# Gathering expert values by token and weighing them in 32-column matmul groups

## Chip, cores, metric

The kernel runs on one core of a Trainium2 chip. The metric is the device time of one execution, in microseconds (us), the median of the runs. Engines are called PE (matmuls), DVE (vector), ACT (scalar), POOL (GpSimd, which here issues the indirect DMAs) and SP (plain DMAs).

## What is computed

One step of a decoder layer for 1024 prompt tokens and 32 sample tokens. The change lies in the expert part alone:

```python
def peer(u, w_pq, sub_keys, exp_u, exp_v):        # 1056 tokens in blocks of 128
    q = (xb @ w_pq).reshape(128, 8, 2, 128)       # 8 heads, two half keys
    s = einsum('thpd,pnd->thpn', q, sub_keys)     # scores against 2 x 128 sub keys
    sv, si = lax.top_k(s, 16)
    comb = sv[:, :, 0, :, None] + sv[:, :, 1, None, :]
    cidx = si[:, :, 0, :, None] * 128 + si[:, :, 1, None, :]
    tv, ti = lax.top_k(comb, 16)
    eidx = take_along_axis(cidx, ti)              # 16 experts per token and head
    g = softmax(tv)
    ue, ve = exp_u[eidx], exp_v[eidx]             # rows of 1024 floats, of 16384 experts
    a = gelu(einsum('td,thkd->thk', xb, ue))
    return einsum('thk,thkd->td', g * a, ve)
```

Each token needs 128 rows of `exp_u` and 128 rows of `exp_v` (8 heads of 16 slots), 4 KB a row.

## The kernel before

The program is a row of stages, each closed by a barrier: loading, attention, convolution, merge, then `experts` (line 1486), then a last normalisation and output. `experts` works through tiles of 128 tokens, eight for the prompt. Token t of a tile sits in partition t. The 32 sample tokens are laid out four times over the partitions, each copy with two of the eight heads, so that the last tile needs only two heads' worth of rounds. That makes 66 units (a unit is one head of one tile), each with 16 gathers of `exp_u` and 16 of `exp_v`: 2112 gathers of 128 rows, 524288 bytes each.

For unit q the work is this. `score` (PE, line 1579) multiplies the tile by the head's folded key weights: 8 fp32 matmuls of 256 columns, each two instructions in the trace. `take_scores` (ACT, 1648) copies the bank. `pick` (DVE, 1714 to 1754) finds the best 16 of each half, forms 70 candidates, takes the best 16 and turns them into expert numbers. `gates` (ACT, 1654) takes the exponentials. Picks run a whole tile ahead of the gathers, since `advance_indices` (1766) hands over all eight heads at once.

`head` (POOL) first copies the unit's indices (1538), then issues 16 gathers into the ring `U` and then 16 into the ring `V` (both at line 1545). Both rings have 8 buffers. A gather for slot k brings one row for each of 128 tokens. It may start when the buffer of eight slots ago is free (`u_free`, `v_free`). POOL executes in order.

`dot` (DVE, 1798) multiplies each U buffer by the tokens and sums along the row, one instruction per slot, and releases the buffer. `weights` (ACT) takes the GELU (1659), DVE multiplies by the gates (1802), and ACT then makes a diagonal matrix per slot (1665, ring of 4). `weigh` (PE, 1589) multiplies that 128x128 diagonal by the V buffer: 2 fp32 matmuls of 512 columns per slot, which are four instructions in the trace, and releases the V buffer. The sum for the tile stays in two PSUM banks; `end` closes it (1600), ACT copies it (1671), PE turns it (1605), DVE adds it to `hT` (1808).

On DVE the order is pick of the unit eight ahead, then `dot` of this unit. On PE it is score, then `weigh`. All of this runs in hardware loops (`Fori`), most of it over heads within a tile. Another stage, `sample_attention`, already multiplies with a 32-column stationary operand into four partition quarters of one PSUM bank (line 999).

## Time and profile before

| What | Value |
|---|---|
| median of 3 runs | 5637.24 us (5636.52 to 5650.34) |
| profiled execution, first to last instruction | 5638.5 us |
| first and last gather of the expert stage start | 2003.97 us, 5379.93 us |
| PE, DVE, POOL busy over the span | 68%, 48%, 47% |
| DMA share, 3000 to 5300 us | 0.92, 329 GB/s |

The profile is of one execution. A timeline row gives start, duration, engine, line, operation, output and inputs and the count; the bracket is the idle time of the engine before it and what ended it. "issue" means that nothing the profile shows was waited for. Busy time of POOL for a gather is the time in which it writes the transfer's descriptors, not the transfer.

### The profile page before, as it was taken

Reading aid. Unit: us, or ns where it says so; the run is one execution under the profiler, and the core shown is the slowest. Engines: PE = TensorE matmul, PEld = TensorE weight load, DVE = VectorE, ACT = ScalarE, POOL = GpSimd, SP = SyncE. Lnnn points to the kernel's source line nnn. Section 1 sums busy time; section 2 is a strip of 40 time slices with the busy share of each in tenths; the row PEclk is TensorE's granted clock in tenths of the full one; section 3 lists DMA queues with packets and bytes.
Section 4 is the critical chain, followed back from the end, with each engine's and each line's share of the span. In section 5 each row is a group of like instructions: output and inputs, shape, how many; then the busy total and the mean of one; then the engine's idle time right before and its main releaser. Section 6 shows DMA issues by size and latency. Waiting matters only on the chain. (4 is left out here: it accounts for less than half of the span.)

```text
span 5638.5 us, 57052 instructions
## 1 busy us (share of the span) xinstructions
PE 3830.5 (68%) x14101; PEld 2341.2 (42%) x14101; DVE 2710.5 (48%) x8425; ACT 1038.5 (18%) x2091; POOL 2646.9 (47%) x2596
## 2 busy tenths in 40 slices
PE   6799854554997656676666666766666666766667
PEld 6667831322887523333333333333333333333246
DVE  2233275343112566555655565555555555555433
ACT  2122121111001211122121121121112111121121
POOL 2100222222112056666666666666666666666621
PEclk8855977777998777887888888888888878888879
DMA  2200166663112379999999999999999999999921
GB/s 62 73 23 12 37 227 221 225 237 106 57 46 61 98 253 331 333 327 323 333 331 325 331 328 332 328 327 335 333 324 328 325 329 329 330 328 333 329 90 50
DMA packets 471328, 1331.83 MB, mean 236 GB/s; under 512 B 48641, under 2 KB 141259, under 8 KB 471257
## 3 DMA queue, kind: packets, MB, share of 16 engines
q0 software_dynamic: 326240, 1180.32, 58.3%
q1 hardware_dynamic: 145024, 150.76, 8.7%
q8 instruction: 28, 0.46, 0.0%
q14 instruction: 36, 0.29, 0.0%
HBM read 1307.67 MB, written 23.66 MB: 236 GB/s over the span
## 5 line engine op out<-in xcount | busy, mean ns | idle before, releaser
L1589 PE MATMUL exp_ps_y<-exp_V,exp_diag 128*128 128x512 f32 x4224 | 1978.3, 632 | 1144.0 <-ACT exp_diag L1665 1125.5
L1798 DVE CUSTOM_DVE_ANT_0 exp_U<-exp_U,exp_x 128x1024 f32<-128x1024 f32 x1056 | 1294.4, 1226 | 1179.8 <-DMA exp_U<-in_exp_u,exp_idx_now 1154.9
L1589 PEld LDWEIGHTS exp_ps_y<-exp_V,exp_diag 128*128 128x128 f32 x4224 | 854.2, 204 | 2241.2 <-issue 1925.2
L1545 POOL DMA_INDIRECT exp_V<-in_exp_v,exp_idx_now x1056 | 1055.4, 999 | 735.5 <-PE exp_ps_y L1589 514.0
L1545 POOL DMA_INDIRECT exp_U<-in_exp_u,exp_idx_now x1056 | 1190.4, 1127 | 383.0 <-issue 312.2
L1665 ACT ACTIVATE exp_diag<-all_ident,exp_wt 128x128 f32<-128x128 f32 x1024 | 389.9, 398 | 1186.4 <-PE exp_ps_y L1589 1137.1
L1579 PE MATMUL exp_ps_sc<-ffn_wk,exp_ust 128*128 (+1 forms) x1152 | 276.4, 395 | 36.1 <-ACT exp_scores L1648 36.1
L1659 ACT ACTIVATE exp_act_dots<-exp_dots 128x16 f32<-128x16 f32 x66 | 14.2, 216 | 1384.4 <-DVE exp_dots L1798 1384.4
L1579 PEld LDWEIGHTS exp_ps_sc<-ffn_wk,exp_ust 128*128 128x128 f32 x1152 | 228.0, 199 | 96.6 <-issue 58.0
L1750 DVE SCALAR_TENSOR_TENSOR exp_picked<-exp_iota,exp_tif,exp_cidx 128x70 f32<-128x70 f32 x1152 | 252.8, 290 | 2.6
L999 PE MATMUL satt_ps_o<-satt_pages,satt_kT 128*32 128x512 f32 x512 | 92.8, 889 | 199.7 <-DMA satt_pages<-in_cache_v 197.5
L898 POOL DMA_DIRECT2D satt_pages<-in_cache_v x128 | 69.0, 539 | 249.6 <-issue 244.3
L958 PE MATMUL satt_ps_t<-all_ident,satt_pages 128*128 128x128 f32 x1024 | 130.0, 284 | 75.5 <-DMA satt_pages<-in_cache_k 37.8
L958 PEld LDWEIGHTS satt_ps_t<-all_ident,satt_pages 128*128 128x128 f32 x1024 | 117.0, 147 | 117.1 <-issue 53.6
L854 DVE SCALAR_TENSOR_TENSOR heads_yT<-convin_gp,all_wdw,heads_yT 128x1024 f32<-128x1024 f32 x120 | 153.3, 1278 | 0.0
L414 PE MATMUL merge_ps_b<-merge_x_high,merge_w_high 128*128 128x352 f32 x384 | 128.5, 335 | 28.8 <-POOL merge_w_low L366 28.8
L898 POOL DMA_DIRECT2D satt_pages<-in_cache_k x128 | 69.8, 546 | 165.6 <-issue 160.5
L655 PE MATMUL patt_ps_s<-patt_kh,patt_qh 66*128 66x512 f32 (+2 forms) x192 | 131.5, 823 | 20.8 <-DMA patt_kh<-k_rows 20.8
L364 POOL CAST merge_w_high<-merge_w 128x1024 fp32r<-128x1024 f32 x16 | 20.6, 1285 | 265.8 <-DMA merge_w<-in_w_in 265.8
L1137 POOL MEMSET convin_gp<- 128x120 f32 x1 | 0.2, 203 | 303.5 <-POOLq L116 303.5
L999 PEld LDWEIGHTS satt_ps_o<-satt_pages,satt_kT 128*32 128x32 f32 x512 | 23.9, 161 | 258.6 <-issue 258.6
L415 PE MATMUL merge_ps_b<-merge_x_low,merge_w_high 128*128 128x352 f32 x384 | 123.6, 322 | 0.0
(309 smaller groups left out, 5107.0 us busy)
## 6 DMA issues: line engine op xcount, KB each, us to landing
satt_pages<-in_cache_k SPq DMA_DIRECT2D x128, 256.0 KB, 4.1
satt_pages<-in_cache_k POOLq DMA_DIRECT2D x128, 256.0 KB, 4.3
satt_pages<-in_cache_v SPq DMA_DIRECT2D x128, 256.0 KB, 6.3
satt_pages<-in_cache_v POOLq DMA_DIRECT2D x128, 256.0 KB, 6.4
exp_U<-in_exp_u,exp_idx_now POOLq DMA_INDIRECT x1056, 6.1
exp_V<-in_exp_v,exp_idx_now POOLq DMA_INDIRECT x1056, 5.6
merge_w<-in_w_in SPq DMA_DIRECT2D x16, 512.0 KB, 4.0
keys_w<-in_w_pq SPq DMA_DIRECT2D x16, 512.0 KB, 4.9
```

Of the source, the lines that this page charges most:

```text
L414: pe.matmul(self.bank(j, c), w_high, x_high, start=first, stop=False)
L415: pe.matmul(self.bank(j, c), w_high, x_low, start=False, stop=False)
L655: last = pe.matmul(sbank[n % 2][:, c0:c1], qh[:, b, qb * P:(qb + 1) * P], kh[:, b, c0:c1], start=True, stop=True)
L854: ins = dve.scalar_tensor_tensor(out=y, in0=x, scalar=wc, in1=y, op0=ALU.mult, op1=ALU.add)
L898: eng.dma_start(ring[:, b, p, :], cache[0, ds(page, 1)].rearrange("a k h d -> k (a h d)"))\
L958: last = pe.transpose(tb[c][:, p * P:(p + 1) * P], ring[:, b, p, c * P:(c + 1) * P], sh.ident[:, :])
L1545: pool.indirect_dma_start(buf[:, k % size, :], None, table[0], bass.IndirectOffsetOnAxis(idx_now[:, hh, k:k + 1], 0))\
L1579: last = pe.matmul(scb[:, 0:2 * P].rearrange("p (a n) -> p a n", n=P), ust[:, k, :], wk[:, k, ds(2 * h, 2), :], start=k == 0, stop=k == KD ...
L1589: last = pe.matmul(yb[f][:, :], diag[:, k % ND, :], V[:, k % NV, f * 512:(f + 1) * 512], start=False, stop=False, skip_group_check=True)
L1665: act.activation(diag[:, k % ND, :], ident[:, :], ACT.Copy, scale=wt[:, k:k + 1]).then_inc(e["diag_ready"], 1)
L1750: st.did(dve.scalar_tensor_tensor(out=picked[:, k, :], in0=iota[:, :], scalar=tif[:, k:k + 1], in1=cidx[:, :], op0=ALU.is_equal, op1=ALU.mult,
L1798: dve.tensor_tensor_reduce(out=row, in0=row, in1=xb[:, :], scale=1.0, scalar=0.0, op0=ALU.mult, op1=ALU.add, accum_out=dots[:, k:k + 1]).t ...
```

## The change

Key gathers and dots stay as they are. Value gathers change from "slot k for 128 tokens" to "all 128 slots of one token", so that there are 1056 of them, as many as before. Expert numbers of a tile are transposed on PE (`turn_indices`) and copied to `idxT`, whose column is one token's list. The weights of a tile are transposed in the same way (`turn_weights`), and one ACT instruction per tile (`spread_weights`) writes them into `spread`, 4 groups of 32 matrices of 128x32 with one column that isn't zero. `weigh` now takes four tokens at once: 2 halves by 4 groups, each a matmul of 128x32 by 128x512 into its quarter of the bank. The diagonals, their 1056 ACT instructions and the copies of scores and indices fall away.

Everything is unrolled and ordered by ticks n of 16 slots. In tick n POOL alternates one key gather of unit n and one value gather, which is 136 gathers behind (`LAG`). PE does the score of unit n + 2, then four groups of `weigh`. ACT copies that score, then takes the GELU of unit n - 1 and the exponentials of unit n + 2. DVE does the pick of unit n + 2, the weights of unit n - 1, then the dots of unit n. The sample tile keeps two units; the four groups of its scores are now 32-row matmuls.

```diff
-    NU, NV, ND = 8, 8, 4
-    U0, V0, G0 = NU, NV + TOPK, 1
+    NU, NV = 8, 8
+    LEAD = 2
+    LAG = P + 8
     NC_ = 70
-
     blocks = [(0, 2, 16), (2, 8, 5), (8, 16, 1)]
+    NUNIT = PH * NT + 2
+    NROW = TOPK * NUNIT
+    NTOK = P * NT + NS
+    NTICK = (NTOK + LAG + TOPK - 1) // TOPK
+
+    def tile_of(n):
+        return min(n // PH, NT)
+
+    def last_unit(t):
+        return min(PH * t + PH, NUNIT) - 1
+
+    def tokens_to(t):
+        return min(P * t + P, NTOK)
...
+        spread = s.sb("spread", [P, 4, NS * NS])
         ysb = s.sb("y", [P, D])
-        scb = s.ps("sc")
+        scb, tb = s.ps("sc"), s.ps("t")
         xt = [s.ps(f"x{i}") for i in range(2)]
-        yb = [s.ps(f"y{i}") for i in range(2)]
...
+        yb = [[s.ps(f"y{b}{f}") for f in range(2)] for b in range(2)]
...
+        def v_begin(t):
+            return (P * t + LAG) // TOPK
+
+        def v_tick_of_end(t):
+            return (tokens_to(t) - 1 + LAG) // TOPK
+
+        def y_tick(t):
+            return v_tick_of_end(t) + 1
...
-            def head(n, col, hh):
-                hold(pool, e["v_free"], V0 + TOPK * (n - 1), e["passed_p"])
-                pool.tensor_copy(idx_now[:, hh, :], idx_cur[:, col]).then_inc(e["staged"], 1)
-                hold(pool, e["staged"], n + 1, e["passed_p"])
-                for table, buf, ring, free, first, size in ((io["exp_u"], U, u_in, e["u_free"], U0, NU),
-                                                            (io["exp_v"], V, v_in, e["v_free"], V0, NV)):
-                    for k in range(TOPK):
-                        if k % 2 == 0:
-                            hold(pool, free, TOPK * n + k + 1 + first - size + 1, e["passed_p"])
-                        pool.indirect_dma_start(buf[:, k % size, :], None, table[0],
-                                                bass.IndirectOffsetOnAxis(idx_now[:, hh, k:k + 1], 0))\
-                            .then_inc(ring[k % size], 16)
...
+            def gather_u(n, k):
+                r = TOPK * n + k
+                if k == 0:
+                    pool.wait_ge(e["idx_ready"], n + 1)
+                if r >= NU:
+                    pool.wait_ge(e["u_free"], r - NU + 1)
+                h = n - PH * tile_of(n)
+                pool.indirect_dma_start(U[:, r % NU, :], None, io["exp_u"][0],
+                                        bass.IndirectOffsetOnAxis(idx[:, tile_of(n) % 2, h * TOPK + k:h * TOPK + k + 1], 0))\
+                    .then_inc(u_in[r % NU], 16)
+
+            def gather_v(v):
+                t, j = min(v // P, NT), v - P * min(v // P, NT)
+                if j == 0:
+                    pool.wait_ge(e["idxT_ready"], t + 1)
+                if v >= NV:
+                    pool.wait_ge(e["v_free"], v - NV + 1)
+                each = NS if t < NT else NS // 4
+                token = each * (j % 4) + j // 4
+                pool.indirect_dma_start(V[:, v % NV, :], None, io["exp_v"][0],
+                                        bass.IndirectOffsetOnAxis(idxT[:, t % 2, token:token + 1], 0))\
+                    .then_inc(v_in[v % NV], 16)
+
+            for n in range(NTICK):
+                for k in range(TOPK):
+                    if n < NUNIT:
+                        gather_u(n, k)
+                    v = TOPK * n + k - LAG
+                    if 0 <= v < NTOK:
+                        gather_v(v)
...
-            def weigh(n):
-                for k in range(TOPK):
-                    g = TOPK * n + k
-                    pe.wait_ge(e["diag_ready"], G0 + g + 1)
-                    pe.wait_ge(v_in[k % NV], 16 * ((TOPK // NV) * n + k // NV + 1))
-                    for f in range(2):
-                        last = pe.matmul(yb[f][:, :], diag[:, k % ND, :], V[:, k % NV, f * 512:(f + 1) * 512],
-                                         start=False, stop=False, skip_group_check=True)
-                    last.then_inc(e["v_free"], 1)
...
+            def turn_indices(t):
+                pe.wait_ge(e["idx_ready"], last_unit(t) + 1)
+                if t >= 1:
+                    pe.wait_ge(e["spread_made"], t)
+                turn_small(t, ef, 0).then_inc(e["idx_turned"], 1)
+
+            def turn_weights(t):
+                pe.wait_ge(e["w_ready"], last_unit(t) + 1)
+                pe.wait_ge(e["idxT_ready"], t + 1)
+                turn_small(t, wt, P).then_inc(e["w_turned"], 1)
+                pe.wait_ge(e["spread_made"], t + 1)
+
+            def weigh(v):
+                t, m = min(v // P, NT), (v - P * min(v // P, NT)) // 4
+                final = m == (NS if t < NT else NS // 4) - 1
+                for g in range(4):
+                    pe.wait_ge(v_in[(v + g) % NV], 16 * ((v + g) // NV) + 16)
+                if m == 0 and t >= 2:
+                    pe.wait_ge(e["y_copied"], t - 1)
+                for f in range(2):
+                    for g in range(4):
+                        x = pe.matmul(yb[t % 2][f][g * NS:(g + 1) * NS, :], spread4[:, g, m, :], V[:, (v + g) % NV, f * 512:(f + 1) * 512],
+                                      start=m == 0, stop=final, skip_group_check=True)
+                        if f == 1:
+                            x.then_inc(e["v_free"], 1)
+                if final:
+                    pe.wait_ge(e["v_free"], tokens_to(t))
+                    pe.sem_inc(e["y_ready"], 1)
...
+            for n in range(LEAD):
+                score(n)
+            for n in range(NTICK + 1):
+                if n + LEAD < NUNIT:
+                    if tile_of(n + LEAD) != tile_of(n + LEAD - 1):
+                        turn_tokens(tile_of(n + LEAD))
+                    score(n + LEAD)
+                for t in range(NT + 1):
+                    if n == last_unit(t):
+                        turn_indices(t)
+                    if n == y_tick(t):
+                        turn_sums(t)
+                for k in range(TOPK):
+                    v = TOPK * n + k - LAG
+                    if 0 <= v < NTOK:
+                        if v % P == 0:
+                            turn_weights(v // P)
+                        if v % 4 == 3:
+                            weigh(v - 3)
...
+                act.activation(sc[:, n % 2, :, :], scb[:, 0:2 * P].rearrange("p (m n) -> p m n", n=P), ACT.Copy)\
...
-            def weights(n, ident, ahead=None):
-                act.wait_ge(e["u_free"], U0 + TOPK * n + TOPK)
-                act.activation(act_dots[:, :], dots[:, :], ACT.Gelu).then_inc(e["gelu_done"], 1)
-                act.wait_ge(e["w_ready"], n + 1)
-                for k in range(TOPK):
-                    if k == ND and ahead is not None:
-                        take_scores(*ahead)
-                    act.wait_ge(e["v_free"], V0 + TOPK * n + k - ND + 1)
-                    act.activation(diag[:, k % ND, :], ident[:, :], ACT.Copy, scale=wt[:, k:k + 1]).then_inc(e["diag_ready"], 1)
...
+            def spread_weights(t):
+                act.wait_ge(e["w_turned"], t + 1)
+                act.wait_ge(e["spread_zeroed"], 1)
+                if t >= 1:
+                    act.wait_ge(e["v_free"], P * t)
+                each = NS if t < NT else NS // 4
+                act.activation(spread[:, :, 0:(each - 1) * (NS + 1) + 1:NS + 1],
+                               tb[:, P:P + 4 * each].rearrange("p (g m) -> p g m", g=4), ACT.Copy).then_inc(e["spread_made"], 1)
...
+            for n in range(NTICK + 1):
+                if n + LEAD < NUNIT:
+                    if tile_of(n + LEAD) != tile_of(n + LEAD - 1):
+                        take_tokens(tile_of(n + LEAD))
+                    take_scores(n + LEAD)
+                if 1 <= n <= NUNIT:
+                    gelu(n - 1)
+                if n + LEAD < NUNIT:
+                    gates(n + LEAD)
+                for t in range(NT + 1):
+                    if n == v_begin(t):
+                        spread_weights(t)
+                    if n == v_tick_of_end(t):
+                        take_sums(t)
...
-                hold(dve, e["gate_done"], q + 1, e["passed_v"])
-                hold(dve, e["sc_copied"], q + 2, e["passed_v"])
-                st.link(dve.tensor_copy(s1[:, :, :], sc[:, ds(2 * h, 2), :]))
...
+            def dot(n):
+                t = tile_of(n)
+                dve.wait_ge(e["xb_copied"], 2 * t + 2)
                 for k in range(TOPK):
-                    dve.wait_ge(u_in[k % NU], 16 * ((TOPK // NU) * n + k // NU + 1))
-                    row = U[:, k % NU, :]
-                    dve.tensor_tensor_reduce(out=row, in0=row, in1=xb[:, :], scale=1.0, scalar=0.0, op0=ALU.mult,
-                                             op1=ALU.add, accum_out=dots[:, k:k + 1]).then_inc(e["u_free"], 1)
-                hold(dve, e["gelu_done"], n + 2, e["passed_v"])
-                hold(dve, e["diag_ready"], G0 + TOPK * n, e["passed_v"])
-                dve.tensor_tensor(wt[:, :], gate[:, col], act_dots[:, :], ALU.mult).then_inc(e["w_ready"], 1)
-
-            def add_sums(t, tok, n):
+                    r = TOPK * n + k
+                    dve.wait_ge(u_in[r % NU], 16 * (r // NU) + 16)
+                    row = U[:, r % NU, :]
+                    dve.tensor_tensor_reduce(out=row, in0=row, in1=xb[:, t % 2, :], scale=1.0, scalar=0.0, op0=ALU.mult,
+                                             op1=ALU.add, accum_out=dots[:, n % 2, k:k + 1]).then_inc(e["u_free"], 1)
+
+            def weights(n):
+                t, h = tile_of(n), n - PH * tile_of(n)
+                dve.wait_ge(e["gate_done"], n + 1)
+                st.link(dve.reciprocal(grec[:, n % 4:n % 4 + 1], gsum[:, n % 4:n % 4 + 1]))
+                dve.wait_ge(e["gelu_done"], n + 1)
+                if t >= 2:
+                    dve.wait_ge(e["w_turned"], t - 1)
+                dve.scalar_tensor_tensor(out=wt[:, t % 2, h * TOPK:(h + 1) * TOPK], in0=act_dots[:, n % 2, :],
+                                         scalar=grec[:, n % 4:n % 4 + 1], in1=ge[:, n % 4, :],
+                                         op0=ALU.mult, op1=ALU.mult).then_inc(e["w_ready"], 1)
+
+            def take_indices(t):
+                dve.wait_ge(e["idx_turned"], t + 1)
+                if t >= 2:
+                    dve.wait_ge(e["v_free"], tokens_to(t - 2))
+                w = P if t < NT else NS
+                dve.tensor_copy(idxT[:, t % 2, 0:w], tb[:, 0:w]).then_inc(e["idxT_ready"], 1)
...
+            for n in range(LEAD):
+                pick(n)
+            for n in range(NTICK + 1):
+                if n + LEAD < NUNIT:
+                    pick(n + LEAD)
+                if 1 <= n <= NUNIT:
+                    weights(n - 1)
+                for t in range(NT + 1):
+                    if n == last_unit(t):
+                        take_indices(t)
+                    if n == y_tick(t):
+                        add_sums(t)
+                if n < NUNIT:
+                    dot(n)
```

## Rows read from the trace of the kernel before

**Rows 1.** The page: busy share by engine over the span.
```profile
PE 3830.5 (68%) x14101; PEld 2341.2 (42%) x14101; DVE 2710.5 (48%) x8425; ACT 1038.5 (18%) x2091; POOL 2646.9 (47%) x2596
```

**Rows 2.** Windows: engines' busy time and counts, granted clock, DMA share, GB/s.
```profile
3447.00:3477.00 30.00, 13.74 (x34) 7.21 (x33) 24.34 (x77) 2.56 (x8) 20.18 (x19) 0.72 0.95 363
3497.00:3529.00 32.00, 14.01 (x36) 7.42 (x35) 25.20 (x77) 2.89 (x9) 22.22 (x21) 0.68 0.92 351
3528.00:3541.00 13.00, 13.00 (x32) 5.78 (x31) 3.61 (x33) 3.12 (x8) 7.48 (x9) 1.00 0.79 261
3548.00:3579.00 31.00, 12.90 (x33) 6.79 (x32) 23.66 (x65) 2.56 (x8) 19.95 (x19) 0.67 0.98 380
3565.00:3570.00 5.00, 0.00 (x0) 0.00 (x0) 4.82 (x9) 0.00 (x0) 3.78 (x5) 0.50 1.03 416
3599.00:3635.00 36.00, 16.92 (x44) 8.72 (x44) 27.50 (x92) 3.36 (x10) 27.32 (x23) 0.76 0.91 326
3651.00:3681.00 30.00, 18.00 (x50) 9.37 (x49) 25.11 (x68) 6.62 (x14) 20.85 (x19) 0.77 0.97 372
3000.00:5300.00 2300.00, 1525.86 (x3704) 729.95 (x3704) 1305.99 (x4513) 438.07 (x1007) 1548.47 (x1484) 0.83 0.92 329
```

**Rows 3.** Timeline of POOL: gathers of the first unit, one in the middle, the last.
```profile
2003.97 1.13 POOL L1545 DMA_INDIRECT exp_U<-in_exp_u,exp_idx_now  x1 [1.06 <-issue]
...
3579.19 0.94 POOL L1545 DMA_INDIRECT exp_V<-in_exp_v,exp_idx_now  x1 [5.00 <-PE exp_ps_y L1589]
...
3582.62 0.94 POOL L1545 DMA_INDIRECT exp_V<-in_exp_v,exp_idx_now  x1 [1.23 <-PE exp_ps_y L1589]
...
5330.96 0.97 POOL L1545 DMA_INDIRECT exp_U<-in_exp_u,exp_idx_now  x1 [0.90 <-POOL exp_idx_now L1538]
```

**Rows 4.** Groups of instructions, 2030 to 5300 us: busy time, mean ns | idle before.
```profile
L1798 DVE CUSTOM_DVE_ANT_0 exp_U<-exp_U,exp_x 128x1024 f32<-128x1024 f32 x1020 | 1250.9, 1226 | 1148.7 <-DMA exp_U<-in_exp_u,exp_idx_now 1124.5
L1545 POOL DMA_INDIRECT exp_U<-in_exp_u,exp_idx_now x1023 | 1151.6, 1126 | 369.4 <-issue 302.0 <-POOL exp_idx_now L1538 62.8 <-DVE exp_dots L1798 4.6
L1545 POOL DMA_INDIRECT exp_V<-in_exp_v,exp_idx_now x1024 | 1024.6, 1001 | 713.4 <-PE exp_ps_y L1589 498.9 <-issue 214.6
```

**Rows 5.** Line 1545: time from a gather's issue to its landing, all 2112.
```profile
DMA to landing us min/median/max: 4.1/6.0/8.3
```

**Rows 6.** Timeline of PE: weigh and score of one unit.
```profile
3520.80 30.16 PE L1589 MATMUL exp_ps_y<-exp_V,exp_diag 128*128 128x512 f32 x64 [17.99 <-ACT exp_diag L1665]
3550.79 3.62 PE L1579 MATMUL exp_ps_sc<-ffn_wk,exp_ust 128*128 x16
```

**Rows 7.** Timeline of PE in sample attention: 32-column matmuls in four quarters.
```profile
903.06 5.92 PE L999 MATMUL satt_ps_o<-satt_pages,satt_kT 128*32 128x512 f32 x32 [13.71 <-DMA satt_pages<-in_cache_v]
```

**Rows 8.** Timeline: hand over of the first scores, first two picks, a score.
```profile
1917.16 1.28 ACT L1648 ACT_TABLE_LOAD   x1 [4.25 <-PE exp_ps_sc L1579]
1918.46 0.38 ACT L1648 ACTIVATE exp_scores<-exp_ps_sc 128x256 f32 x1
1919.09 0.29 DVE L1714 COPY exp_s<-exp_scores 128x256 f32 x1 [11.22 <-ACT exp_scores L1648]
...
1929.89 0.49 DVE L1717 MAX8 exp_sv<-exp_s 128x8 f32<-128x128 f32 x2
1937.33 5.97 PE L1579 MATMUL exp_ps_sc<-ffn_wk,exp_ust 128*128 x16 [4.39 <-ACT exp_scores L1648]
1938.77 0.17 DVE L1754 CAST exp_idx_next<-exp_ef 128x16 f32 x1
```

**Rows 9.** Timeline of DVE: two dots back to back.
```profile
3554.26 1.23 DVE L1798 CUSTOM_DVE_ANT_0 exp_U<-exp_U,exp_x 128x1024 f32<-128x1024 f32 x1
...
3555.53 1.23 DVE L1798 CUSTOM_DVE_ANT_0 exp_U<-exp_U,exp_x 128x1024 f32<-128x1024 f32 x1
```

**Rows 10.** Timeline at the end of the stage: last gather and last add.
```profile
5379.93 0.95 POOL L1545 DMA_INDIRECT exp_V<-in_exp_v,exp_idx_now  x1 [0.30 <-issue]
...
5395.36 0.73 DVE L1808 TENSOR_TENSOR all_hT<-exp_ps_x,all_hT 128x128 f32<-128x128 f32 x2 [34.37 <-PE exp_ps_x L1605]
```

301 lines of the change are left out of this document (107 added, 194 removed).

## Prediction, made before the changed kernel was run

> **What bounds the kernel now.** The page's first part comes first [rows 1]: no engine is busy for more than 68% of the span, so the limit is a transfer or a chain of waits. Next the windows [rows 2]: through the expert stage the DMA engines have a share of 0.92 and move 329 GB/s. It isn't a flat ceiling, though: 261 GB/s in one stretch, 416 in another, and the slow stretch is the one in which PE is busy all of the time. The timeline of POOL says why [rows 3]. POOL issues 24 gathers freely, about 1.25 us apart at best (0.94 of work and 0.30 between). Then it waits 5.00 us for the first V buffer of the unit, and from there 1.23 us for every second one. Each pair of V gathers then takes 3.43 us (3582.62 - 3579.19), which is two slots of `weigh` (30.16 us for 16 slots, its first few slow, [rows 6]). So a unit is part DMA limited and part PE limited. It takes (5330.96 - 2003.97) / 65 = 51.2 us [rows 3]; the groups show 499 us of POOL's waiting for PE in all, and DVE waits 1124 us for U rows, so it has room [rows 4].
>
> **The sum.** The stage is the only one touched, and it starts and ends at barriers, so what it saves is saved. I place its last gather, now at 5379.93 us [rows 10], in four parts.
>
> *Start.* The first pick starts at 1919.1 [rows 8], unchanged, since tokens and first score are loaded as before. A pick without its copy takes 9.06 us (1929.89 to 1938.94, [rows 8]). The new order does three picks before the first dot: 1919.1 + 3 x 9.1 + 0.3 = 1946.7. POOL needs only the first pick for its first gather, so it starts near 1929 and no longer at 2004; the buffers are full when DVE comes.
>
> *Keys alone.* For 8.5 ticks there are no V gathers. Dots follow each other by 1.28 us [rows 9]. A tick on DVE is 16 x 1.28 = 20.5, a pick 9.06, and 0.5 for reciprocal and weights (an estimate, two small operations like the cast of 0.17 with their waits, [rows 8]): 30.0 us. This bounds the tick, since 16 gathers at 1.47 us need 23.5. Dot row 8 of unit 8, which lets the first pair go, ends at 1946.7 + 8 x 30.0 + 1.3 = 2188 us.
>
> *Pairs.* 920 keys and 920 values remain in pairs, 57.5 ticks of 32 gathers. Four limits on a tick:
> DMA. Free stretches of five successive units (30 to 36 us each, 326 to 380 GB/s) have a time-weighted mean of 357 GB/s [rows 2]. That is 0.524 MB / 357 GB/s = 1.47 us a gather, 47.0 us a tick. The bounds are 1.26 us (416 GB/s) and 1.61 us (326 GB/s), so 40 to 51.5 us.
> POOL. 0.30 + 1.126 (keys) and 0.30 + 1.001 (values) [rows 4]: 43.6 us a tick, below DMA. It was stretched beside dots, and dots now lie beside both kinds. All at the keys' 1.126 it would be 45.6.
> PE. Four groups of tokens and a score. A 512-column instruction takes 3.43 / 8 = 0.43 us at 2.4 GHz (two slots of `weigh`, four instructions each, clock at 1.00 in the stretch from 3528, [rows 2, 3]). No row shows `weigh` in its new form, but [rows 7] has the same form in another stage: 32 instructions in 5.92 us, where one after the other they would take 13.7 at 2.4 GHz. Four at a time are 8 rounds, 3.4 us at 2.4 and 6.9 at 1.2 GHz, and 5.92 lies between. So the quarters run beside each other, and a `weigh` of 16 instructions is 4 rounds, 1.7 or 3.4 us. At the lower clock PE has 4 x 3.4 + 6.0 = 19.6 us of work in a tick and isn't the bound. Without that concurrency a `weigh` would take 6.9 us at 2.4 and 13.7 at 1.2 GHz; I take the row of the same shape.
> The chain. This is what the change adds: PE's queue is in order, so the score of unit n + 2 stands behind the last `weigh` of tick n - 1, and DVE's first instruction of tick n, the pick, waits for that score. Weights, dots and thereby free U buffers stand behind the pick, and POOL, in order too, holds V gathers behind a U gather that waits. From the landing of the last U row: V row behind it 1.4, `weigh` 3.4, score 4.1, PE to ACT 0.3, a possible table load 1.3 (1.28 in [rows 8]), copy and hand over 0.6 (1918.46 to 1919.09), pick 9.1, weights 0.5, first dot 1.3, hand over 0.1: 22.1 us. For the score I take 4.1 as it lies behind 3.4 us of PE work: a score after an idle PE took 5.97 us, one behind a long `weigh` 3.62 [rows 6, 8]. The ends are 18.5 (all at 2.4 GHz, no load) and 25 us. From there 14 more issues to the last U gather at 1.25 to 1.3 and its landing at 6.0 [rows 5]: 22.1 + 18.2 + 6.0 = 46.3 us; ends 42.7 and 49.2. At the DMA pace POOL would ask for that U buffer at -6.0 + 18 x 1.47 = 20.5 us, so it waits 1.6 us while four gathers (6.0 / 1.47) are in flight, and the DMA engines don't run dry.
> DMA at 47.0 and chain at 46.3 nearly tie, so what varies in either adds; I take 47.5 us a tick, 2731 us in all. At eight tile changes a turn of the tokens stands in the chain (2 us each): 16 us. End of pairs: 2188 + 2731 + 16 = 4935.
>
> *Values alone.* 136 gathers are left. Buffers come free by fours, so eight gathers need a landing and a weigh twice over: 3 more issues at 1.27 and a landing of about 5.2 (between 4.1 and 6.0, [rows 5]) + 3.4 + 0.3 to the next, which makes 12.7 us for eight, 1.6 us each. That is 218 us, last gather at 5153. Before it was at 5379.93: 227 us less. What follows the last gather took 16.2 us [rows 10] and loses the diagonals and a closing product: about 1 us less.
>
> Diagonals (18% of the span is all that ACT is busy, [rows 1]), index copies and per-loop restarts leave engines that weren't late. Their removal is counted at nothing, except where the copy leaves the pick. The transposes per tile (two small ones, one ACT write to `spread`) lie under 11.8 us between groups of four tokens; without that cover they would be some 3 us x 9. The unrolled code is longer, and I count no loading of it.
>
> Together 5638.5 - 228 = 5410 us. The profiled execution is within 1.3 us of the median, so that is the prediction for the median too: time = 5410 + 57.5 x (tick - 47.5).
>
> A rule against the sum. The rows show gathers stretched to 1.126 us beside dots and 1.001 for values, many of which lie beside picks. The Trainium skill ("SBUF — State Buffer", on the port pair shared by VectorE and GpSimd) says that a VectorE operation with two SBUF inputs locks out a GpSimd operation that reads SBUF for its whole length. A full block of half a dot (0.6 us) for each of the 14 or so gathers beside dots would make POOL's tick 32 x 1.25 + 14 x 0.6 = 48.4 us, an estimate, and the kernel 5462; the keys' mean is 0.19 us above the shortest work of 0.94 [rows 3, 4], which speaks against the full block.
>
> **Rivals.**
> A. *The DMA engines are at their limit already.* A share of 0.92 may be all that mixed gathers reach; the slow free stretch (326 GB/s) is as slow as the mean. Then a tick stays near 51.2 us and only start and end change: 5410 + 57.5 x 3.7 = 5623, and with a tick of 49.5, 5525. Against it: 363 and 416 GB/s in other stretches.
> B. *Slower: the chain wins.* In its place, the score behind `weigh`, anything that lengthens PE's part moves the tick one to one. The tick exceeds 51.2 us when the chain to the first dot exceeds 27 us, that is when weigh and score together take over 12.4 us and not 7.5; from 51.5 the kernel is slower than before. With the quarters one after the other at 1.2 GHz it is 13.7 + 6.0: chain 34.3 us, tick 58.5, kernel 6043. For it: PE now works in short bursts, and its granted clock was 0.50 (1.2 GHz) in a stretch without PE work [rows 2]. Against it: [rows 7].
> C. *Faster.* If the DMA engines hold 416 GB/s when always fed, POOL or the chain's short end is the bound at 43.6 us: 5410 - 224 = 5186.
> The Trainium skill ("HBM Reference", its note on the two cores of a domain) gives about 425 GB/s for a core that streams alone; that is case C, and by it an estimate of 39.5 us for a tick's transfers, under POOL's. The rows hold such a rate only for 5 us.
> D. *The change doesn't do what it says*: no change of rate in the pairs, because POOL still waits for PE. It is A in time and would show as V gathers waiting for PE.
>
> **Chances.** Forecast (tick of 45.5 to 49.5 us, 5295 to 5525): 0.62. A and D (5525 to 5655): 0.17, of which 0.05 above 5620. B (above 5655): 0.12. C (below 5295): 0.09. The range takes in forecast and A, with their edges: 5290 to 5630, which leaves 2 in 10 out. A measurement of this kernel can tell about 0.3%, 17 us. Faster by more (below 5620): 0.62 + 0.12 + 0.09 = 0.83; within: 0.05; slower: 0.12.
>
> **What would show it.** First gather near 1929 us; nine ticks of 30 us with DVE busy throughout; then gathers alternating, 1.47 us apart on average, POOL's waits for PE gone from the V gathers and a wait of 1 to 3 us for a dot at the ninth U gather of each tick; DMA share 0.95 or more; `weigh` of 16 instructions in 3.4 us; last gather near 5153. Wrong if the pairs' tick is above 49.5: then a wait of POOL for dots of 4 us or more means the chain, and no wait but long issues means the DMA engines. The sum also fails if the key phase isn't DVE bound.

## The result, and the profile after

The changed kernel takes 5941.72 us (median of 4 runs, 5932.57 to 5957.04), the kernel before took 5640.24 us beside it. The ratio is 1.0529, with a 95% interval of 1.0498 to 1.056: slower by 5.3%, where 4% less was forecast. The profiled execution has a span of 5943.5 us.

Page, one window of the pair phase, and the groups from 2030 to 5300 us (as [rows 1, 2, 4]):

```profile
PE 2762.0 (46%) x14061; PEld 1654.2 (28%) x14061; DVE 2580.3 (43%) x7980; ACT 630.6 (11%) x1018; POOL 2811.8 (47%) x2530
3000.00:5300.00 2300.00, 740.99 (x3354) 252.08 (x3354) 1142.33 (x4084) 155.27 (x265) 1493.61 (x1298) 0.61 0.81 297
L1563 POOL DMA_INDIRECT exp_U<-in_exp_u,exp_idx x958 | 1088.6, 1136 | 878.6 <-DVE exp_dots L1815 605.0 <-issue 273.6
L1575 POOL DMA_INDIRECT exp_V<-in_exp_v,exp_idxT x873 | 1031.2, 1181 | 272.9 <-issue 265.3 <-PE exp_ps_y L1647 4.0 <-remote 3.6
```

The DMA share fell from 0.92 to 0.81 and the rate from 329 to 297 GB/s [rows 2]. POOL's 499 us of waiting for PE are gone, as meant; 605 us of waiting for a dot stand in their place. That points to the chain: the row of steps in which each waits for the one before and which brings the tick to its end. One tick (start, length, wait before, for POOL, DVE, PE and ACT):

```profile
3977.59 0.94 POOL L1563 DMA_INDIRECT exp_U<-in_exp_u,exp_idx  x1 [0.30 <-issue]
3983.63 1.23 DVE L1815 CUSTOM_DVE_ANT_0 exp_U<-exp_U,exp_x 128x1024 f32<-128x1024 f32 x1 [2.07 <-DMA exp_U<-in_exp_u,exp_idx]
3985.00 3.37 PE L1647 MATMUL exp_ps_y<-exp_V,exp_spread 128*32 128x512 f32 x16 [7.28 <-DMA exp_V<-in_exp_v,exp_idxT]
3988.30 3.72 PE L1608 MATMUL exp_ps_sc<-ffn_wk,exp_ust 128*128 128x256 f32 x16
3993.15 0.38 ACT L1699 ACTIVATE exp_scores<-exp_ps_sc 128x256 f32<-128x256 f32 x1 [43.99 <-PE exp_ps_sc L1608]
3993.57 0.49 DVE L1762 MAX8 exp_sv<-exp_scores 128x8 f32<-128x128 f32 x2 [8.71 <-issue]
3998.80 0.23 DVE L1789 MAX8 exp_tv<-exp_cand 128x8 f32<-128x70 f32 x1 [1.49 <-DVE exp_cidx L1783]
4001.61 0.09 DVE L1790 MATCH_VALUE_LOAD exp_ti<-exp_tv,exp_cand 128x8 f32 x1 [2.58 <-remote]
4009.50 1.68 POOL L1563 DMA_INDIRECT exp_U<-in_exp_u,exp_idx  x1 [8.84 <-DVE exp_dots L1815]
4011.49 1.99 POOL L1575 DMA_INDIRECT exp_V<-in_exp_v,exp_idxT  x1 [0.30 <-issue]
4053.36 0.59 PE L1647 MATMUL exp_ps_y<-exp_V,exp_spread 128*32 128x512 f32 x1 [1.15 <-issue]
4057.61 0.38 ACT L1699 ACTIVATE exp_scores<-exp_ps_sc 128x256 f32<-128x256 f32 x1 [45.82 <-remote]
```

The last key gather starts at 3977.59, its dot at 3983.63; weigh and score follow, the pick starts at 3993.57, and POOL goes on at 4009.50 after 8.84 us of waiting. Some things weren't in the forecast: waits of 1.5 and 2.6 us inside the pick, before steps whose inputs VectorE itself had written (the first also waits for exponentials of two units earlier, long done); gathers of 1.7 to 2.0 us beside the dots; and, in the tick after this one, a copy of the scores at 4057.61, some 9 us after its score was done, and PE waiting 1.15 us for nothing visible between two instructions of one `weigh`.

From the timelines of the profiled executions I took the same steps for the 50 ticks of units 12 to 61, as means in us. "To score" runs from the start of the last dot to the start of the score, "copy" from the start of the score to ACT's copy, "pick" from its first step to the start of its last, "14 issues" from the ninth key gather of the tick to the sixteenth, seven keys and seven values (the recorded expectations call this stretch eight pairs):

| | landing | to score | copy | pick | 14 issues | tick | time |
|---|---|---|---|---|---|---|---|
| forecast | 6.0 | 4.8 | 5.7 | 9.1 | 18.2 | 46.3 (chain) | 5410 |
| after | 6.25 | 5.14 | 7.81 | 11.98 | 23.06 | 56.7 | 5942 |
| paced only (p0) | 5.93 | 5.15 | 4.06 | 9.02 | 24.82 | 53.3 | 5780 |
| dot gap (e3) | 6.15 | 5.15 | 13.1 | 9.6 | 20.28 | 56.8 | 5954 |
| small values (e4) | 4.48 | 4.27 | 8.82 | 13.06 | 23.90 | 57.0 | 5946 |
| score early (e1) | 6.14 | - | - | 20.06 | 23.08 | 52.6 | 5693 |

The rest of a tick, about 2.5 us (4.3 in p0, where POOL's fills delay the ninth key), is handing over, weights and the first dot. The changed kernel's row adds up: 6.25 + 5.14 + 7.81 + 0.42 + 11.98 + 0.60 + 1.49 + 23.06 = 56.75, and the forecast's own formula with it, 5410 + 57.5 x (56.75 - 47.5), gives 5942. That it fits to the microsecond is partly luck, as the last part of this document shows.

### The profile page after: what moved, and what is told of

Same layout as the page of the kernel before. It is cut to its first block and busy times, and to the rows that moved or that the text cites. A ratio compares the mean times of both kernels' runs of the same rounds, so it can differ in the third digit from the quotient of the medians.

```text
span 5943.5 us, 48298 instructions
## 1 busy us (share of the span) xinstructions
PE 2762.0 (46%) x14061; PEld 1654.2 (28%) x14061; DVE 2580.3 (43%) x7980; ACT 630.6 (11%) x1018; POOL 2811.8 (47%) x2530
## 5 line engine op out<-in xcount | busy, mean ns | idle before, releaser
L1647 PE MATMUL exp_ps_y<-exp_V,exp_spread 128*32 128x512 f32 x4224 | 910.6, 1001 | 2315.1 <-DMA exp_V<-in_exp_v,exp_idxT 2260.1
L1563 POOL DMA_INDIRECT exp_U<-in_exp_u,exp_idx x1056 | 1205.1, 1141 | 967.2 <-DVE exp_dots L1815 648.4
L1815 DVE CUSTOM_DVE_ANT_0 exp_U<-exp_U,exp_x 128x1024 f32<-128x1024 f32 x1056 | 1251.9, 1222 | 795.7 <-DMA exp_U<-in_exp_u,exp_idx 793.7
L1575 POOL DMA_INDIRECT exp_V<-in_exp_v,exp_idxT x1056 | 1216.6, 1152 | 393.5 <-issue 315.9
L1647 PEld LDWEIGHTS exp_ps_y<-exp_V,exp_spread 128*32 128x32 f32 x4224 | 178.0, 153 | 2962.5 <-issue 2962.0
L1608 PE MATMUL exp_ps_sc<-ffn_wk,exp_ust 128*128 128x256 f32 x1024 | 279.8, 433 | 164.6 <-ACT exp_scores L1699 134.7
L1762 DVE MAX8 exp_sv<-exp_scores 128x8 f32<-128x128 f32 x132 | 32.1, 285 | 695.8 <-issue 373.4
L1699 ACT ACTIVATE exp_scores<-exp_ps_sc 128x256 f32<-128x256 f32 x66 | 25.1, 380 | 2281.6 <-remote 973.0
L1801 DVE SCALAR_TENSOR_TENSOR exp_picked<-exp_iota,exp_tif,exp_cidx 128x70 f32<-128x70 f32 x1056 | 230.0, 289 | 3.4 <-DVE exp_picked L1801 1.0
L416 PE MATMUL merge_ps_b<-merge_x_high,merge_w_low 128*128 128x352 f32 x384 | 124.1, 323 | 0.0
```

The costliest lines, as they stand in the source:

```text
L1563: pool.indirect_dma_start(U[:, r % NU, :], None, io["exp_u"][0], bass.IndirectOffsetOnAxis(idx[:, tile_of(n) % 2, h * TOPK + k:h * TOPK + ...
L1575: pool.indirect_dma_start(V[:, v % NV, :], None, io["exp_v"][0], bass.IndirectOffsetOnAxis(idxT[:, t % 2, token:token + 1], 0))\
L1608: last = pe.matmul(scb[:, 0:2 * P].rearrange("p (a n) -> p a n", n=P), ust[:, k, :], wk[:, k, 2 * h:2 * h + 2, :], start=k == 0, stop=k == ...
L1647: x = pe.matmul(yb[t % 2][f][g * NS:(g + 1) * NS, :], spread4[:, g, m, :], V[:, (v + g) % NV, f * 512:(f + 1) * 512], start=m == 0, stop=f ...
L1801: st.did(dve.scalar_tensor_tensor(out=picked[:, k % 4, :], in0=iota[:, :], scalar=tif[:, k:k + 1], in1=cidx[:, :], op0=ALU.is_equal, op1=A ...
L1815: dve.tensor_tensor_reduce(out=row, in0=row, in1=xb[:, t % 2, :], scale=1.0, scalar=0.0, op0=ALU.mult, op1=ALU.add, accum_out=dots[:, n % ...
```

## Experiments

### Is it the chain or the bytes?

**e1**, the score moved out of the chain:

```diff
-                if n + LEAD < NUNIT:
-                    ...
-                    score(n + LEAD)
+                    if k == 8 and n + LEAD + 1 < NUNIT:
+                        ...
+                        score(n + LEAD + 1)
```

> The changed kernel with one thing moved: PE scores unit n+3 (and turns its tile's tokens) behind the second weigh of tick n instead of scoring unit n+2 at the head of tick n, and ACT copies those scores at the end of its tick. Nothing is left out. Chain theory: in the changed kernel each tick of pairs (56.8 us) is one chain, and 5.3 us from the last dot to the score, 7.6 us from the score to ACT's copy and 0.4 us to the pick stand in it, 13.3 us together; with the scores ready ahead of the pick they drop out, the tick would fall to about 43.5 us, where POOL's and the DMA queue's own 44 to 47 us take over: about 47 us, so 5942 - 55 x 9.8 = about 5400 us (5330 to 5480). DMA theory (the sixteen pairs of a tick can't be moved in less than they take now, the waits only fill the time): stays within 1% of 5942 us, and the wait moves to another place.

Measured: 5693 us (1.0097 of before, 1.0063 to 1.0132), tick 52.6 us, where about 47 was expected. The score left the chain, but of the 13.3 us only 4.1 came: the pick went from 12.0 to 20.1 us. Its last steps, each 0.3 us of work (VectorE's timeline, e1):

```profile
3552.26 0.29 DVE L1803 SCALAR_TENSOR_TENSOR exp_picked<-exp_iota,exp_tif,exp_cidx 128x70 f32<-128x70 f32 x1 [0.65 <-DVE exp_picked L1803]
3553.70 0.29 DVE L1803 SCALAR_TENSOR_TENSOR exp_picked<-exp_iota,exp_tif,exp_cidx 128x70 f32<-128x70 f32 x1 [1.14 <-DVE exp_picked L1803]
3554.39 0.08 DVE L1803 DVE_READ_ACCUMULATOR exp_picked<-exp_iota,exp_tif,exp_cidx 128x1 f32 x1 [0.40 <-issue]
3555.13 0.29 DVE L1803 SCALAR_TENSOR_TENSOR exp_picked<-exp_iota,exp_tif,exp_cidx 128x70 f32<-128x70 f32 x1 [0.65 <-DVE exp_picked L1803]
```

Undisturbed, these sixteen steps are 0.21 us apart. Here three follow each other at 1.4 us.

**e4**, the same orders and waits with an eighth of the values' bytes, so that most of the values' part of the sums is left out (`V` is filled with zeros once ahead of the stage, which moves the first gather from 1925 to 1950 us):

```diff
-                pool.indirect_dma_start(V[:, v % NV, :], None, io["exp_v"][0],
+                pool.indirect_dma_start(V[:, v % NV, 0:128], None, io["exp_v"][0].rearrange("e (a b) -> (e a) b", b=128),
```

> The changed kernel with value gathers of an eighth of the bytes: each row brings 128 columns instead of 1024, the other 7/8 of V's columns stay zero, so the values' part of the sums is left out for the most part; all instructions, orders and waits are those of the changed kernel. DMA load falls by nearly half. Chain theory: the landing of the last key comes 2 to 4 us sooner, else the chain of 56.8 us per tick stands: tick 51 to 55 us, total about 5620 to 5850 us. DMA theory: tick falls by the bytes, to 35 to 45 us, total below 5300 us. Of the stalls: if VectorE's 2.3 to 2.6 us stalls within the pick and ScalarE's 9 to 10 us ones ahead of the score's copy come from the load on the DMA queues, they vanish (pick back to 8.9 us, score to copy 3.8 us, which alone would make the tick 7 us shorter: about 5550 us); if they come from GpSimd's dense issue of gathers, they stay, though at other places. If the key gathers of 1.7 to 2.0 us come from a full queue they fall to 0.94 us; if from the dots beside them they stay.

Measured: 5946 us (one run), tick 57.0. The row of the same window shows a DMA share of 0.56 and 167 GB/s:

```profile
3000.00:5300.00 2300.00, 729.25 (x3345) 248.64 (x3347) 1129.06 (x4055) 155.69 (x265) 1512.50 (x1289) 0.61 0.56 167
```

So bytes neither hold this tick nor cause the stalls. The landing is 1.8 us shorter and the way to the score 0.9; copy, pick and the 14 issues grew by 1.0, 1.1 and 0.8 and took that back. I had expected 5620 to 5850 even by the chain: a miss that turned the search to GpSimd's issue.

**e2**, only the alternation undone:

```diff
                 for k in range(TOPK):
-                    if n < NUNIT:
-                        gather_u(n, k)
                     v = TOPK * n + k - LAG
                     if 0 <= v < NTOK:
                         gather_v(v)
+                for k in range(TOPK):
+                    if n < NUNIT:
+                        gather_u(n, k)
```

> The changed kernel, but POOL issues the sixteen value gathers of a tick first and its sixteen key gathers after them: the alternation alone is undone, with the same work. Chain theory (the score stands behind the four weighs of a tick, and these behind the last value, which is issued after the last key): the last value of a tick now lands some 16 issues ahead of the last key, so the weighs (5.3 us) are done when the last dot ends, the score and its copy overlap the dots and the pick starts at the last dot; the chain is then last landing, pick 9 to 12, dot 1.2, then 8 value and 8 key issues of which only the first 8 keys of the next tick wait: tick about 46 to 50 us, total about 5400 to 5570 us. DMA theory: within 1% of 5942 us. If the order of the gathers were good in itself (alternation evens out what each engine has to do), it is slower than 5942 us.

Measured: 5500 us (0.975, 0.9721 to 0.9778), tick 48.9, 2.5% faster than before. Undoing the alternation alone takes off 7.4%: it had put the last value, and with it weigh and score, behind the last key. **e12**, e1 and e2 together:

> The first two edits together on the changed kernel: PE scores a unit one tick earlier, behind the second weigh, and POOL issues a tick's sixteen value gathers ahead of its sixteen key gathers. Nothing is left out. With values first alone (5500 us) the tick was 48.9 us and the pick still waited 6.5 us on average for the score's copy, and took 13.3 us instead of 8.9. Chain theory: the 6.5 us drop out too and the tick falls to 43 to 45 us: about 5300 us. Issue theory (VectorE's and ScalarE's steps slow down once GpSimd has issued some eight gathers back to back, by about 0.7 us for each instruction, whatever the bytes): the pick now lies fully beside dense issue, takes 15 to 22 us, and eats the gain: 5450 to 5650 us.

Measured: 5400 us (0.9574, 0.9536 to 0.9612), tick 47.2, pick 12.2. That is between the two expectations and a miss of both: the pick neither came back to 9 us nor grew to 15, and the tick stopped above 43 to 45 us.

### The port

**e3**, a gap between dots, as each now waits for the semaphore of the one before:

```diff
                     r = TOPK * n + k
+                    if k:
+                        dve.wait_ge(e["u_free"], r)
```

> The changed kernel with one wait added: each dot of a unit waits until the one before it has written its semaphore, as dots of the kernel before are apart by more (1.28 us there, 1.15 us here back to back). Port theory (GpSimd's gathers beside back-to-back dots take 1.69 to 1.99 us instead of 0.94 because VectorE holds the port that they share, and the eight pairs of issues from dot 0 to the last key take 23.05 us where 18.2 were expected): a gap after each dot lets GpSimd in, gathers beside dots fall to 1.0 to 1.3 us, the stretch falls to 19 to 20 us, and each of 55 ticks by 3 to 4 us: about 5740 us. Rival (the long gathers come from the full DMA queue, not from VectorE): gathers beside dots stay at 1.7 to 2.0 us, time within 0.5% of 5942 us or up to 1% more for the dots' own gaps.

Measured: 5954 us, no gain where about 5740 was expected. Gathers that lie wholly within a row of back-to-back dots have a mean of 1.86 us in the changed kernel (280 of them, median 1.99); with the gap (dots 1.38 us apart) it is 1.17 (577). The 14 issues fell from 23.06 to 20.28. But the copy went from 7.8 to 13.1 us and ate this and what the pick gave. That the denser issue makes the stalls longer fits; this run alone doesn't show it. Where the order lets it through, the gap counts. **e23**, values first with the gap:

> Values first and a gap between dots (each dot waits for the semaphore of the one before). Nothing is left out. With values first alone POOL was issuing 48 us of each 48.9 us tick, 8 us of it because gathers beside back-to-back dots took 1.7 to 2.0 us. Port theory: these fall to 1.0 to 1.3 us, POOL's tick falls to 42 to 44 us, the DMA queue's 41 to 47 us take over: tick 44 to 47 us, total 5280 to 5430 us. Rival (what the gap gives comes back as longer stalls of pick and copy, since GpSimd now issues more densely, as it did when the gap was added alone: 5954 against 5942 us): 5480 to 5560 us.

Measured: 5393 us (0.9567, 0.952 to 0.9614), 107 us less than e2. All three edits, **e123**:

> Score early, values first, and the gap between dots, all three on the changed kernel. Any two of them with values first gave 5393 and 5400 us (tick 47.2 us). If the tick is now held by what each gather costs behind GpSimd (1.41 us each, 45.1 us a tick) it can still fall to 45 to 46 us: 5280 to 5340 us. If it is held by the bytes at 1.47 us a gather, as in the kernel before, it stays at 47 us: 5385 to 5405 us.

Measured: 5399 us (0.9558, 0.9532 to 0.9583), tick 47.4.

### The stalls

**probe_stalls** puts small stages ahead of the expert stage. In all but the first ("quiet", with no gathers) GpSimd gathers while VectorE and ScalarE copy one column over and over:

> The changed kernel with five small stages put in ahead of the expert stage, which leave its data alone; only they are read. In each VectorE copies one column 400 times, in turns four without a semaphore and four that each wait for their own, and ScalarE copies one column 150 times without a semaphore, beside gathers of GpSimd: none (quiet); 32 back to back of 64 KB (small); 20 back to back of 512 KB (wide); 32 of 64 KB with VectorE's copies in a loop and none waiting (loop); 32 of 64 KB with a fill of 128 columns after each (paced). Issue theory: after some eight gathers both small and wide slow VectorE and ScalarE down to about 0.7 us a step, loop too, paced not. DMA theory (full DMA engines delay semaphores and code): wide slows, small doesn't. Code theory: small and wide slow, loop doesn't. Semaphore theory: only the copies that wait are slow. Port theory: each gather holds VectorE up but not ScalarE, from the first gather on.

The GpSimd and ScalarE parts of a stage:

```python
for i in range(gathers):
    pool.indirect_dma_start(G[:, i, :], None, table, bass.IndirectOffsetOnAxis(at[:, i:i + 1], 0)).then_inc(landed, 16)
...
for i in range(3 * NR):
    act.activation(c[:, i:i + 1], zero[:, :], ACT.Copy)
```

Stage "small" (64 KB gathers from 1963.3 to 2003), windows of 4 us: at its beginning, in the middle, and after the end; then "wide" and "loop" in their middle. Counts are in brackets behind DVE and ACT:

```profile
1966.00:1970.00 4.00, 0.00 (x0) 0.00 (x0) 3.42 (x35) 2.84 (x30) 3.08 (x4) 0.50 0.17 51
1990.00:1994.00 4.00, 0.00 (x0) 0.00 (x0) 0.40 (x5) 0.61 (x3) 3.09 (x4) 0.50 0.20 59
2010.00:2014.00 4.00, 0.00 (x0) 0.00 (x0) 3.45 (x33) 2.40 (x26) 0.00 (x0) 0.50 0.00 0
2066.00:2070.00 4.00, 0.00 (x0) 0.00 (x0) 0.70 (x7) 0.61 (x3) 2.99 (x4) 0.50 1.03 411
2139.00:2143.00 4.00, 0.00 (x0) 0.00 (x0) 0.46 (x3) 0.72 (x4) 3.08 (x4) 0.50 0.17 49
```

ScalarE in the middle of "small", no semaphore in its stream:

```profile
1988.78 0.20 ACT L1533 ACTIVATE small_c<-small_zero 128x1 f32<-128x1 f32 x1 [1.19 <-issue]
1990.18 0.20 ACT L1533 ACTIVATE small_c<-small_zero 128x1 f32<-128x1 f32 x1 [1.20 <-issue]
1991.58 0.20 ACT L1533 ACTIVATE small_c<-small_zero 128x1 f32<-128x1 f32 x1 [1.20 <-issue]
```

The first idle times on ScalarE come some 5 us after the first gather, as the fifth is issued. They grow until, in the middle of the stage, ScalarE is at a tenth of its pace (one instruction in 1.40 us) and VectorE at a seventh. In "small" the last gather has been issued by 2003.2 us, and both engines come back to their pace only 5 us later. Bytes (share 0.17 or 1.03), loop or straight code, and semaphores make no difference, and ScalarE is hit as VectorE is. The quiet stage has no such idle time. ScalarE is back 45.1 us after the first of 32 gathers, 28.2 us after the first of 20, and 45.1 us with a fill (pitch 1.34 us): 1.41 us a gather each time. So something behind an indirect gather takes 1.41 us; at an issue of 1.25 us it piles up, and VectorE and ScalarE slow down with it. That the paced stage would be free of stalls was a miss: the fill was too short.

**probe_pitch** looks for the pitch and the port:

> The changed kernel with seven small stages ahead of the expert stage, which leave its data alone; only they are read. As in the first probe, GpSimd issues gathers of 64 KB while VectorE copies one column 400 times and ScalarE 150 times: 32 gathers back to back (fill0), with a fill of 256 (fill256) and of 384 columns (fill384) after each, and 5 and 10 gathers back to back. Issue theory: a service of 1.41 us a gather; fill0 (pitch 1.25) stalls from the sixth gather until 45.1 us after the first; fill256 (about 1.45) and fill384 (about 1.55) don't stall; five ends before stalls begin, ten stalls for a few us and ends 14.1 us after its first. If fill256 and fill384 stall as well, the pitch isn't what decides. In the last two stages VectorE works back to back on 1024 columns, with two inputs in SBUF (two) and with one (one), beside 16 gathers. Port theory: gathers beside two take 1.7 to 2.0 us as beside the kernel's dots, beside one 0.95 us; if both or neither lengthen them, it isn't the second input.

Middle of 32 gathers at 1.25, at 1.44 and at 1.55 us, then the gathers beside two-input and beside one-input work of VectorE (min, median, max ns):

```profile
1936.00:1940.00 4.00, 0.00 (x0) 0.00 (x0) 0.25 (x5) 0.61 (x3) 2.91 (x4) 0.50 0.16 49
2016.00:2020.00 4.00, 0.00 (x0) 0.00 (x0) 3.45 (x35) 0.00 (x0) 3.52 (x6) 0.50 0.17 49
2070.00:2074.00 4.00, 0.00 (x0) 0.00 (x0) 3.45 (x33) 0.00 (x0) 3.68 (x6) 0.50 0.12 33
L1505 POOL DMA_INDIRECT two_G<-in_exp_u,two_at x16: 943/1887/1972, 2208.3 to 2236.1; - x16
L1505 POOL DMA_INDIRECT one_G<-in_exp_u,one_at x16: 943/1017/1286, 2243.1 to 2262.8; - x16
```

At 1.25 us VectorE does 5 copies in 4 us, at 1.44 and 1.55 us 35 and 33, as many as at the quiet beginning of "small". (ScalarE shows none in these two windows because it had already finished; it had no idle time over 0.4 us in either stage.) Ten gathers back to back held ScalarE until 14.2 us after the first. Five held it until 7.1 us, 1.41 us for each again: that five would end before stalls begin was a miss. The last rows are medians of all 16 gathers. Those wholly beside VectorE's work take 1.82 to 1.97 us with two inputs in SBUF, and 1.02 us (the first 1.29) with one; the seven behind the work take 0.94 in both.

**probe_packets** asks what costs the 1.41 us:

> The changed kernel with five small stages ahead of the expert stage, which leave its data alone; only they are read. VectorE copies one column 400 times and ScalarE 200 times beside 32 gathers of 512-byte rows, of 128 rows (full), 64 (half) and 32 (quarter), and beside 64 plain transfers of 128 rows of 512 bytes issued by GpSimd (plain) and by SyncE (sync). A gather of 128 rows cost 1.41 us behind its issue, that is 11 ns a row. Per-row theory: half and quarter need 0.70 and 0.35 us, less than any pitch of issue, and nothing stalls; plain and sync stall if their rows come faster than one in 11 ns. Per-gather theory: half and quarter stall like full, 45 us. GpSimd theory: full stalls, perhaps plain, and sync never does, however fast its rows come.

```profile
L1535 ACT ACTIVATE full_c<-full_zero x200: 186/188/203, 1901.9 to 1955.8; 128x1 f32<-128x1 f32 x100
L1535 ACT ACTIVATE quarter_c<-quarter_zero x200: 186/188/203, 2071.0 to 2126.4; 128x1 f32<-128x1 f32 x100
L1535 ACT ACTIVATE plain_c<-plain_zero x200: 186/188/203, 2156.7 to 2175.3; 128x1 f32<-128x1 f32 x100
L1535 ACT ACTIVATE sync_c<-sync_zero x200: 187/188/203, 2207.7 to 2226.3; 128x1 f32<-128x1 f32 x100
```

ScalarE's 200 copies take 18.6 us beside plain transfers of either engine, one each 0.5 us, and 54 to 55 us beside gathers, of 128 rows or of 32. All three sizes hold it until 44.8 to 45.0 us after the first. It is a price of each indirect gather, not of rows, bytes or transfers as such.

### The stalls in the kernel

**p0**, the changed kernel with GpSimd slowed down and nothing else:

```diff
+        def fill(pool):
+            issued.append(1)
+            for i in range(1 + (len(issued) % 2 == 0)):
+                ...
+                pool.memset(rest[:, :], 0.0).then_inc(e["filled"], 1)
```

> The changed kernel with nothing moved, only GpSimd paced: after each gather it fills a tile of 128 columns, after every second one twice, each fill waiting for the one before, so that undisturbed gathers start some 1.45 to 1.5 us apart instead of 1.25. In the stages put in before, other engines' steps slowed down until 1.41 us for every gather had passed (32 gathers in 45.1 us, 20 in 28.2 us). Issue theory with that price: at a pitch over 1.41 us nothing piles up, the pick falls from 12.0 to 9 us and the time from the score to its copy from 7.8 to 4 to 5 us, against some 2 to 4 us more from the eighth to the last key gather: tick 52 to 55 us instead of 56.8, total 5700 to 5850 us although 2112 gathers each cost more. Rival (the stalls aren't set by the pitch): pick and copy as before, the longer pitch comes on top, 6050 to 6150 us.

Measured: 5780 us (1.0236, 1.021 to 1.0261), 2.7% less than the changed kernel, though 3168 fills were added. All 50 picks lie between 8.9 and 9.3 us. The copy, and the beginning and end of a pick:

```profile
3960.12 0.38 ACT L1712 ACTIVATE exp_scores<-exp_ps_sc 128x256 f32<-128x256 f32 x1 [30.25 <-PE exp_ps_sc L1621]
3960.53 0.49 DVE L1775 MAX8 exp_sv<-exp_scores 128x8 f32<-128x128 f32 x2 [7.72 <-issue]
3969.57 0.20 DVE L1818 CAST exp_idx<-exp_ef 128x16 int32<-128x16 f32 x1
```

This settles the stalls: 7.81 - 4.06 of the copy and 11.98 - 9.02 of the pick, 6.7 us a tick. The tick fell by 3.4 only, as the fills lengthen the 14 issues by 1.8 and the way from the first dot to the ninth key by 1.7 us. **p1**, e1 with one fill after each gather:

> Score early, as in the first experiment (5693 us, where the pick took 20.1 us instead of 8.9), with GpSimd paced: after each gather it fills a tile of 128 columns and waits for that before the next fill, so that gathers start about 1.5 to 1.6 us apart instead of 1.25. Nothing is left out. Issue theory (the stalls of the pick come from gathers issued back to back faster than something behind them drains): the pick falls to 9 to 12 us though as many gathers lie beside it; the tick becomes POOL's own 32 x 1.55 = 50 us and the eight longer ones, 50 to 56 us, total 5550 to 5850 us. Port theory alone (each gather beside the pick holds it up) or a loading of code: the pick stays at 18 us or more, and the total goes up to 5800 us or more.

Measured: 5578 us (one run), tick 50.0, pick 13.1 instead of 20.1. The median pitch of the gathers (from the start of one to the start of the next) is 1.34 us and not the 1.5 to 1.6 expected, still below 1.41. **p12**, e12 with p0's fills:

> Score early and values first together (5400 us, tick 47.3 us), with the same pace of GpSimd. Issue theory: no stalls of pick and copy, the tick is POOL's 32 x 1.47 = 47 us or the DMA queue's 47 us: 5380 to 5450 us, pick 9 us where it was 12.0 on average with the longest at 20. Rival (at 47 us the tick is already at the DMA queue's limit, 358 GB/s at a share of 0.95, as in the kernel before): no change, 5400 us, whatever the pick does.

Measured: 5874 us (1.0392, 1.0324 to 1.0461), a miss of both theories. The pick is 9.0 us, so the stalls are gone, but e12 has too little slack on POOL, some 6 us of waiting in a tick of 47: each gather with its gaps now takes 1.10 + 0.51 us instead of 0.98 + 0.31, which is 10 us a tick. Tick 55.0.

### What holds the 47 us

**e124**, e12 with small values:

> Score early and values first together (5400 us, tick 47.2 us, DMA share 0.95 at 358 GB/s), with value gathers of an eighth of the bytes: each row brings 128 of 1024 columns, the rest of V stays zero, so the values' part of the sums is left out for the most part. Bytes theory (47 us a tick is 32 gathers of 1.47 us of the DMA engines): the bytes fall to 0.56 of what they were, the tick falls to what is next, the 1.41 us a gather that the probes showed behind GpSimd's issue, 45.1 us, or less: about 5230 to 5300 us, some 80 us of it from the last 136 values, which then need 1.41 instead of 1.6 us or less. Issue theory (GpSimd's service and the stalls it causes hold the tick, bytes don't): the tick stays at 46.5 to 47.5 us and the total at 5350 to 5400 us, as small values changed nothing in the changed kernel (5946 against 5942 us).

Measured: 5352 us (0.9498, 0.9479 to 0.9517), tick 47.25. The tick is of the profiled execution, the slowest of five (5386 us); by the other four it would be some 0.6 us less, an estimate. From 3000 to 4900 us, where both are in their pairs, e124 moves 202 GB/s and e12 357, in ticks of the same length, so bytes aren't the floor: nearly half of them are worth 0.9% of the time, or 1.4% without the fill of `V` ahead of the stage (first gather at 1950 us, in e12 at 1924). The row of the usual window, which here takes in the end of the stage:

```profile
3000.00:5300.00 2300.00, 874.69 (x4607) 355.74 (x4608) 1244.61 (x4111) 187.24 (x301) 1608.06 (x1479) 0.68 0.53 178
```

**f1** and **f13**: score early, gathers by fours, without and with the gap.

```diff
+                for q in range(4):
+                    for k in range(4 * q, 4 * q + 4):
+                        ... gather_v(v)
+                    for k in range(4 * q, 4 * q + 4):
+                        ... gather_u(n, k)
```

> Score early, and the gathers of a tick by fours: four values, four keys, four values and so on, instead of one by one (5693 us, pick 20 us) or all sixteen values first (5400 us, tick 47.2 us). Nothing is left out. With all values first GpSimd waits 340 us in all for a weigh, since eight value buffers are used up in a burst; small values showed that bytes don't hold the tick. Ring theory (the burst of values against a ring of eight holds the 47.2 us): by fours that wait goes and a tick falls to 45 to 46 us, the 1.41 us a gather of the probes: 5290 to 5350 us. Issue theory (the sum of gathers lengthened by dots and of stalls holds it, in whatever order, as the steps of pick slow down when GpSimd no longer pauses): 5390 to 5560 us, with a pick of 14 us or more.

> The same by fours with the gap between dots. Ring theory: as before or up to 50 us less, 5280 to 5340 us. Issue theory: the gap makes gathers beside dots shorter, GpSimd denser and the stalls of the pick longer; the two cancel, within 1% of the version without the gap.

Measured: 5670 us (1.0032, 1.0009 to 1.0054) and 5413 us (0.958, 0.9551 to 0.961), ticks of 52.4 and 47.6 us. Both expectations missed in both runs: by fours is slower than all values first, and the gap changed 4.5% where it was to change nothing or 1%. At least the ring of value buffers isn't what holds 47 us. The pick takes 23.3 and 22.3 us; that the gap alone then makes 4.8 us a tick is the price of dots back to back at its clearest (14 issues 19.2 against 14.8 us). Four versions with all bytes stop at 47.2 to 47.6 us (e12, e23, e123, f13). 32 gathers of 1.41 us are 45.1 us. That this service and the stalls it causes are the floor fits, but 2 us are left over and no run removed it: it stays open.

## Why the prediction was wrong

**The direction.** The forecast was that PE's limit goes and that DMA and the chain, at 47.0 and 46.3 us a tick, nearly tie. The step that failed is the chain's 46.3 us: its terms for pick, copy and the 14 issues were each too small, and the chain took 56.75. That PE's limit goes is right: hardly a wait for PE is left, `weigh` mostly takes 3.4 to 3.6 us as forecast from [rows 7] for the lower clock, the first gather is at 1925.2 us (1929 forecast), and the landing is 6.25 (6.0). Rival B (slower, the chain wins) had the place and its threshold of 27 us to the end of the first dot: 5.1 + 7.8 + 0.4 + 12.0 + 0.6 + 1.5 = 27.4. Its mechanism, quarters one after the other, was not it: most of what came on top lay in pick and copy. Even so 27.4 us alone would give only 51.6 us a tick; the rest came from the 14 issues.

**Pick and copy, 9.1 and 5.7 us.** Taken from rows at the stage's start [rows 8], when no gather had been issued (the first starts at 2003.97 us). Measured 12.0 and 7.8. The price of the new order is that 16 gathers are issued freely while pick and score wait in line, and gathers issued under 1.41 us apart hold up VectorE and ScalarE. In the kernel before, units took 51.2 us for 32 gathers. The 24 that were issued without a wait took 1.43 us each on average, some of them lengthened by dots, and the pick stood where POOL waited for PE:

```profile
3522.64 0.49 DVE L1717 MAX8 exp_sv<-exp_s 128x8 f32<-128x128 f32 x2
3527.73 0.94 POOL L1545 DMA_INDIRECT exp_V<-in_exp_v,exp_idx_now  x1 [3.99 <-PE exp_ps_y L1589]
3531.58 0.17 DVE L1754 CAST exp_idx_next<-exp_ef 128x16 f32 x1
```

There every pick took 8.8 to 9.2 us. It fits that the waits which the change removed had kept the pick short: in p0, with slower issue alone, it is short again. The row that should have warned is [rows 3]: 0.30 + 0.94 us is faster than anything the stage had kept up.

**Fourteen issues at 1.25 to 1.3 us, 18.2 us.** Measured 23.06. The first four of them lie beside eight back-to-back dots and take 1.69, 1.97, 1.99 and 1.99 us on average, the other ten 0.94 to 1.32. I had weighed the rule of the Trainium skill ("SBUF — State Buffer", port pair shared by VectorE and GpSimd) and set it aside, since the mean of [rows 4] was 1.126 us. That mean was of other dots: before, they stood 1.28 us apart [rows 9], and the 562 gathers wholly within rows of them took 1.13 us on average, half of them 0.98 or less. The unrolled dots stand 1.15 us apart, with no idle time between, and the gathers take 1.86. The probe's two-input and one-input stages, 1.97 and 1.02 us, agree with the rule. My estimate by it, 0.6 us for each of 14, was wrong both ways: a gather beside such dots takes 1.0 us more, but only some four or five of them in a tick are. Of the 4.9 us missed in this term, 3.6 lie in the first four.

**Keys alone, 30.0 us a tick.** Measured 32.2: dots closer together, but the last rows of a tick late, as their gathers, beside the dots, took 1.7 to 2.0 us. The first value gather came at 2207 us and not at 2188.

**Values alone, 1.6 us each.** Measured 1.73, 18 us in all. This and the 19 us of the key phase aren't in the formula; they are made up by the eight tile changes (16 us in the forecast), which the measured mean of 56.75 already holds, and by the pairs outside the 50 ticks, which were a little shorter (16 us more). So the formula's 5942 us is right in the tick and lucky in the rest.

**"The DMA engines don't run dry."** I let a nearly tied chain overlap with four gathers in flight. POOL's wait at the ninth key was 10.5 us on average (3.5 to 16.0) and not 1.6, which is more than a landing, and the share fell to 0.81.

**DMA, 47.0 us a tick.** The size looks right, since the best versions stop there, but the reason is wrong (e124). The engines can also do more than the 357 GB/s it was taken from: in e2, gathers ran at 406 GB/s from 3612 to 3626 us.

```profile
DMA packets 1559, 5.69 MB, mean 406 GB/s; under 512 B 171, under 2 KB 171, under 8 KB 1559
```

That is case C's rate, near the 425 GB/s that the Trainium skill gives for a core that streams alone ("HBM Reference", specifications for trn2). It didn't help, as bytes weren't the bound.

Of the 9.25 us missed a tick, then: 4.9 in the 14 issues, 5.0 stalls beyond the slack that I had in these terms (6.7 in full), 0.6 landing and hand over, less 1.2 by which I had put the tick above the chain.

**What the change was worth.** Tokens by four groups with picks two ahead, kept, with values first and a gap between dots, give 5393 us, 4.3% less than before. The alternation was the part that made it slower.

## What to carry to other kernels

Interleaving two gather streams tied the end of one to the end of the other here (e2: 7.4%). Ask what stands behind the last transfer of each, and issue first the stream with the longer tail (here value, weigh, score, copy, pick). Price an engine's steps by rows with the same neighbours as in the new order, not by quiet ones, and look at the longest of a group beside its mean. Ask also what an engine does while another waits: a step can be short because of that wait. When an engine's wait is removed, compute the issue rate that results and compare it with the highest rate that a row shows to be sustained without slowing others.

## What the hardware showed that I had not expected

- An indirect gather of GpSimd takes 0.95 + 0.30 us to issue, but something behind it takes 1.41 us (5, 10, 20 and 32 gathers: 7.1, 14.2, 28.2 and 45.1 us). Issued faster, gathers slow VectorE and ScalarE down from the fifth on, in the middle of 32 to one ScalarE instruction in 1.4 us, until 1.41 us for each has passed. PE showed an idle time of 1.15 us inside a `weigh` beside them; no probe looked at PE. It doesn't depend on rows (32 to 128) or bytes (16 to 512 KB), and plain transfers each 0.5 us don't do it. At a pitch of 1.44 us it is gone. What is used up isn't shown. All runs were profiled, so the recording itself is a rival that no run here excludes: whether the stalls are as long without a profile can't be told from them.
- Two-input VectorE work back to back lengthens a gather from 0.94 to 1.97 us, one-input work to 1.02; dots 1.38 us apart instead of 1.15 avoid most of it.
- The DMA engines kept 406 GB/s over 14 us of gathers of 4 KB rows (e2).
